# Low-rank projections on unnormalised x, a narrow rotary key, merged query rotary parts and a router on VectorE, in a two-layer diffusion step

## What is computed

```
h = rmsnorm(x) * (1 + scale) + shift           # scale, shift from the conditioning
z = h @ w_in  ->  qd, kd, vd (512 each), cq (256), ckv (128), kr (32)
q_mla = rmsnorm(cq) @ w_uq                      # 4 heads x (64 plain + 32 rotary)
ckv   = rmsnorm(ckv); kr = rotary(kr)           # kr is one key part, shared by 4 heads
diff  = softmax(q1 k1) - lam * softmax(q2 k2), times v      # 4 heads
mla   = softmax(qn (ckv w_uk) + qr kr) (ckv w_uv)           # 4 heads
x = x + gate * ([diff, mla] @ w_o)
h = rmsnorm(x) * (1 + scale) + shift
x = x + gate * ffn(h)       # layer 0: SwiGLU 2816 wide; layer 1: best 2 of 8 experts
```

## Time and profile before

| | |
|---|---|
| median of 3 runs | 2214.25 us (2213.64 to 2216.69) |
| profiled execution | 2219.65 us, span 2218.0 us |
| busy in the span | TensorE 95%, its weight loads 83%, VectorE 61%, ScalarE 52%, GpSimd 6% |
| mean granted TensorE clock | 0.987 |
| layer 0 begins, layer 1 begins, router, experts, end | 0, 901, 1291, 1333, 2158 us |

### The profile page before, as it was taken

One profiled execution on the slowest core, in us unless ns is written; L12 is line 12 of the kernel. 1 busy time (PEld: TensorE's weight loads), 2 busy tenths in 40 slices (PEclk: granted clock), 3 DMA queues, 4 the chain that ended last, 5 costly groups with the idle time before them and its releaser, 6 DMA issues. The chain is left out here.

```text
span 2218.0 us, 32258 instructions
## 1 busy us (share of the span) xinstructions
PE 2115.1 (95%) x12409; PEld 1836.0 (83%) x12409; DVE 1353.8 (61%) x1447; ACT 1143.0 (52%) x1419; POOL 127.0 (6%) x147
## 2 busy tenths in 40 slices
PE   5999899999999999899999988999999999999996
PEld 2998567999999999798856877888888888888885
DVE  4427443644423443543843367989998998998884
ACT  3316453322212222422844336787777887877763
POOL 0130100000000000022010030000000000000001
PEclk8999999999999999999999989999999999999998
DMA  8320045256432212312015219999999999999964
GB/s 286 100 83 6 1 152 188 81 164 206 138 91 77 77 55 71 113 58 64 6 39 190 96 68 393 386 387 387 387 387 386 386 387 387 386 387 386 386 247 143
DMA packets 281711, 455.41 MB, mean 205 GB/s; under 512 B 12368, under 2 KB 160720, under 8 KB 281616
## 3 DMA queue, kind: packets, MB, share of 16 engines
q1 hardware_dynamic: 267040, 419.74, 53.8%
q0 software_dynamic: 7920, 28.84, 3.3%
q10 hardware_dynamic: 6656, 5.47, 0.8%
HBM read 426.07 MB, written 27.95 MB: 205 GB/s over the span
## 5 line engine op out<-in xcount | busy, mean ns | idle before, releaser
L1655 DVE TENSOR_TENSOR w_lo<-mraw,w_hi 128x1792 fp32r<-128x1792 f32 (+2 forms) x306 | 642.7, 2111 | 92.6 <-ACT w_hi L1095 91.3
L1095 ACT ACTIVATE w_hi<-mraw 128x1792 fp32r<-128x1792 f32 (+2 forms) x306 | 541.8, 1775 | 189.6 <-PE ps L2272 156.6
L2270 PE MATMUL ps<-w_hi,xs_lo 128*128 128x448 f32 (+1 forms) x816 | 311.2, 381 | 7.3 <-DVE w_lo L1655 6.6
L2272 PE MATMUL ps<-w_hi,xs_hi 128*128 128x448 f32 (+1 forms) x816 | 305.9, 375 | 0.0
L2271 PE MATMUL ps<-w_lo,xs_hi 128*128 128x448 f32 (+1 forms) x816 | 305.6, 375 | 0.0
L1203 DVE TENSOR_TENSOR sub_lo<-zone,sub_hi 128x1024 fp32r<-128x1024 f32 (+2 forms) x114 | 132.0, 1159 | 268.7 <-ACT sub_hi L802 268.6
L802 ACT ACTIVATE sub_hi<-zone 128x1024 fp32r<-128x1024 f32 (+2 forms) x114 | 111.2, 978 | 145.5 <-PE ps L1898 98.8
L2270 PEld LDWEIGHTS ps<-w_hi,xs_lo 128*128 128x128 f32 x816 | 153.7, 188 | 34.0 <-DVE w_lo L1655 14.9
L2272 PEld LDWEIGHTS ps<-w_hi,xs_hi 128*128 128x128 f32 x816 | 153.6, 188 | 19.7
L2271 PEld LDWEIGHTS ps<-w_lo,xs_hi 128*128 128x128 f32 x816 | 153.8, 189 | 18.4
L1375 DVE TENSOR_REDUCE stat<-ps 128x2 f32<-128x1536 f32 (+3 forms) x80 | 92.4, 1157 | 114.1 <-PE ps L1982 97.5
(11 more groups left out here) (291 smaller groups left out, 3566.4 us busy)
## 6 DMA issues: line engine op xcount, KB each, us to landing
mraw<-in_moe_w_down SPq DMA_DIRECT2D x68, 1024.0 KB, 13.6
mraw<-in_moe_w_gate SPq DMA_DIRECT2D x68, 896.0 KB, 13.1
mraw<-in_moe_w_up SPq DMA_DIRECT2D x68, 896.0 KB, 13.3
zone<-in_w_ada SPq DMA_DIRECT2D x48, 1024.0 KB, 5.9
mraw<-in_moe_w_gate SPq DMA_DIRECT2D x34, 1024.0 KB, 14.4
mraw<-in_moe_w_up SPq DMA_DIRECT2D x34, 1024.0 KB, 14.3
mraw<-in_moe_w_down SPq DMA_DIRECT2D x34, 768.0 KB, 13.4
zone<-in_w_in SPq DMA_DIRECT2D x14, 1024.0 KB, 5.4
```

Source lines behind the costliest of these rows:

```text
L1095: nc.scalar.activation(w_hi[:, n % SPLITS, a], mraw[:, n % MRING, a], ACT.Copy).then_inc(w_hi_ready, 1)
L1655: nc.vector.tensor_tensor(w_lo[:, n % SPLITS, a], mraw[:, n % MRING, a], w_hi[:, n % SPLITS, a].bitcast(f32), ALU.subtract).then_inc(w_spl ...
L2270: nc.tensor.matmul(out, a_lo, b_hi, start=start, stop=False)
L2272: return nc.tensor.matmul(out, a_hi, b_hi, start=False, stop=stop)
```

## The change

It does five things.

1. In layer 1 the three low-rank labels take gain times x, which ScalarE and VectorE write chunk by chunk behind the down projections; `make_gain(1, 0)` moves ahead of these. The token sums stand between chunks 4 and 5 of the first label. VectorE multiplies by the token factor as it reads PSUM (`low_rank_scaled`), ScalarE adds the shift (`low_rank_shifted`). `keep_busy` goes. The norm and its split parts are still made, for the labels that follow, and `("rope", 1, 0)` takes them chunk by chunk. In layer 1 the loads of small weights and caches go from ScalarE's queue to GpSimd's.
2. The rotary key is no padded label any more: `key_part` does 32-wide float32 matmuls in four column groups, `key_sums` adds the groups and rotates, VectorE finishes (`key_rope`).
3. The query weights are reordered so that the plain parts of two heads share one label of 128 (`uq`), and the rotary parts of all four heads another (`("rope", l, 8)`, finished by `query_rope`). The `uk` labels cover two heads each. GpSimd copies the key part to the four heads.
4. In the router the five masks become one operation, the shift additions go from GpSimd to VectorE, between its other steps.
5. The router's softmax goes behind the experts.

The diff, cut to its core:

```diff
+            m(("rope", l, r), "raw_ready", 9 * l + r + 1)
+            if r == 0:
+                m(("kr", l), "kr_copied", l + 1)
+            if r == 1:
+                m(("kr_sum", l), "kr_summed", l + 1)
...
-        for h in range(4):
-            x(("rot", l, 9 + h), "rot_used", 13 * l + 10 + h)
-        for r in range(9, 13):
-            m(("rope", l, r), "raw_ready", 13 * l + r + 1)
-        for h in range(4):
-            m(("uk", l, h), "km_ready", 4 * l + h + 1)
+        x(("rot", l, 8), "rot_used", 9 * l + 9)
+        m(("rope", l, 8), "raw_ready", 9 * l + 9)
+        for g in range(2):
+            m(("uq", l, g), "uq_out", 2 * l + g + 1)
+        for g in range(2):
+            m(("uk", l, g), "km_ready", 4 * l + 2 * g + 2)
...
+        def small_weights_in(eng, l):
+            eng.dma_start(wkr, w_in[l, :, :, 1920:1952]).then_inc(layer_w_in[l], 16)
+            eng.dma_start(wuq, d["w_uq"][l].rearrange("(k p) n -> p k n", p=P)).then_inc(layer_w_in[l], 16)
+            eng.dma_start(wuk, d["w_uk"][l]).then_inc(layer_w_in[l], 16)
+            eng.dma_start(wuv, d["w_uv"][l]).then_inc(layer_w_in[l], 16)
+        def caches_in(eng, l):
+            eng.dma_start(ckv_t[:, 0:PAST], d["cache_ckv"][l]).then_inc(cache_c_in[l], 16)
+            eng.dma_start(kr_t[NOPE:MQK, 0:PAST], d["cache_kr"][l]).then_inc(cache_c_in[l], 16)
+            eng.dma_start(k_t[:, :, 0:PAST], d["cache_k"][l]).then_inc(cache_k_in[l], 16)
+            eng.dma_start(v_n[:, 0:2, :], d["cache_v"][l]).then_inc(cache_v_in[l], 16)
         block = ctx.enter_context(nc.Block())
...
             for l in range(DEPTH):
-                for r in range(13):
+                if l:
+                    pool.wait_ge(late_turned, TURNS_BEFORE[l])
+                    pool.wait_ge(main_done, MAIN[("lora", l, 0)] + 1)
+                    small_weights_in(pool, l)
+                    pool.wait_ge(main_done, MAIN[("lora", l, 2)] + 1)
+                    caches_in(pool, l)
+                for r in range(8):
                     rope_item(l, r)
+                pool.wait_ge(kr_done, l + 1)
+                pool.wait_ge(cache_c_in[l], 16 * N_CACHE_C)
+                pool.wait_ge(kv_out, 16 * 4 * (l + 1))
+                pool.wait_ge(scores_done, (2 * l + 1) * ITEMS)
+                for h in range(HEADS):
+                    nc.gpsimd.tensor_copy(k_t[NOPE:MQK, h, :], kr_t[NOPE:MQK, :]).then_inc(kr_spread, 1)
...
-                pool.wait_ge(shift_row_ready, 2)
-                pool.wait_ge(htok_scaled, t + 1)
-                nc.gpsimd.tensor_tensor(htok[:, t, :], htok[:, t, :], shift_row[t // (TT - 1)], ALU.add).then_inc(htok_ready, 1)
...
+                    sub_hi_part(q + 3)
                 else:
...
                     root(4 * l + 1)
                     act.wait_ge(zero_rows, 16 * 2 * XTILES)
-                    modulate(1, 1, 0)
...
+                    modulate(1, 1, 0, ks=range(3))
+                    sub_hi_part(q + 3)
+                    modulate(1, 1, 0, ks=range(3, KC))
+                    sub_hi_part(q + 4)
+                def low_rank_shifted(g):
+                    act.wait_ge(lora_scaled, g + 1)
+                    for c, (a, b) in enumerate(((0, N_LAT), (N_LAT, T))):
+                        ins = nc.scalar.activation(lora_raw[:, g, a:b], lora_raw[:, g, a:b], ACT.Identity,
+                                                   bias=shift_part[:, g // 2, g % 2, c:c + 1])
+                    ins.then_inc(lora_ready, 1)
...
-                    raw_item(l, r)
+                act.wait_ge(scores_done, (2 * l + 1) * ITEMS)
+                for g in range(2):
+                    act.wait_ge(main_done, MAIN[("uq", l, g)] + 1)
+                    for c in range(2):
+                        ins = nc.scalar.activation(q_t[0:NOPE, 2 * g + c, :], main_pair(("uq", l, g))[NOPE * c:NOPE * c + NOPE, :],
+                                                   ACT.Copy, scale=-M_SCALE)
+                    ins.then_inc(uq_out, 1)
...
+                                if d_ == 0:
+                                    act.wait_ge(gain_ready, 4)
+                                for c, (a, b) in enumerate(((0, N_LAT), (N_LAT, T))):
+                                    ins = nc.scalar.activation(f_hi[:, d_, a:b], x_t[:, d_, a:b], ACT.Copy, scale=gain[:, 1, 0, d_, c:c + 1])
+                                ins.then_inc(h_hi_ready, 1)
...

...
+                kr_ps = main_pair(("kr_sum", l))[rows]
+                nc.vector.tensor_copy(kr_t[rows, PAST + N_LAT:NKEY], kr_ps[:, N_LAT:T])
+                nc.vector.tensor_tensor(kr_t[rows, PAST:PAST + N_LAT], kr_ps[:, 0:N_LAT], cos_m[rows, :], ALU.mult).then_inc(kr_summed, 1)
+                dve.wait_ge(aux_done, AUX[("kr_rot", l)] + 1)
+                nc.vector.tensor_tensor(kr_raw[rows, 0:N_LAT], AUXP[rows, 0:N_LAT], sin_m[rows, :], ALU.mult).then_inc(kr_rotated, 1)
+                dve.wait_ge(kr_rotated, l + 1)
+                dve.wait_ge(kr_summed, l + 1)
+                nc.vector.tensor_tensor(kr_t[rows, PAST:PAST + N_LAT], kr_t[rows, PAST:PAST + N_LAT], kr_raw[rows, 0:N_LAT],
+                                        ALU.add).then_inc(kr_done, 1)
...
+            def query_rope(l):
+                n = 9 * l + 8
+                dve.wait_ge(raw_ready, n + 1)
+                dve.wait_ge(rope_done, n)
+                link(nc.vector.tensor_tensor(rtmp[:, (n + 1) % 2, :], raw[:, n % 2, 0:N_LAT], cos_m[:], ALU.mult))
+                rot(l, 8)
+                dve.wait_ge(rot_used, n + 1)
+                dve.wait_ge(scores_done, (2 * l + 1) * ITEMS)
+                for h in range(HEADS):
+                    rows = slice(ROPE * h, ROPE * h + ROPE)
+                    ins = nc.vector.tensor_tensor(q_t[NOPE:MQK, h, 0:N_LAT], rtmp[rows, 0, :], rtmp[rows, 1, :], ALU.add)
+                ins.then_inc(rope_done, 1)
 
...
+                def low_rank_scaled(g):
+                    m = MAIN[("lora", 1, g)]
+                    dve.wait_ge(main_done, m + 1)
+                    nc.vector.tensor_tensor(halves(lora_raw[:, g, :]), main_halves(("lora", 1, g)), halves(rb[:]), ALU.mult)
+                    o = 1024 * (m % 3) + 512 + TH
+                    nc.vector.tensor_copy(shift_part[:, g // 2, g % 2, :], ps[:, o:o + 2]).then_inc(lora_scaled, 1)
+                def beside_norm(k):
+                    if k == 2:
+                        low_rank_scaled(0)
+                    if k == 5:
+                        sub_rest(q + 3)
+                    if k == 7:
+                        low_rank_scaled(1)
                 if l:
                     sub_rest(q + 2)
-                    norm(2 * l, l, 4 * l + 1, ("norm", l, "mix"), 16 * l)
-                sub_rest(q + 3)
-                sub_rest(q + 4)
...
-                    if h == 0:
-                        dve.wait_ge(rope_done, 13 * l + 9)
-                        dve.wait_ge(cache_c_in, 16 * N_CACHE_C * (l + 1))
-                    nc.vector.tensor_copy(k_t[NOPE:MQK, h, :], kr_t[NOPE:MQK, :]).then_inc(kr_spread, 1)
...
+                        if half:
+                            dve.wait_ge(mod_late, TURNS_BEFORE[1])
+                            make_gain(1, 0)
+                            nc.vector.drain().then_inc(gain_ready, 1)
                         for d_ in range(KC):
                             for _ in range(2):
                                 q += 1
@@ -1560,9 +1633,13 @@
                             residual(l, ("down", half, d_), d_, 40)
                             if half and d_:
                                 add_square(1, "mix", d_ - 1)
+                                scaled_rest(d_ - 1, 1, 0)
+                            if half and d_ == 1:
+                                dve.wait_ge(shift_hi, 2)
+                                nc.vector.tensor_tensor(f_lo[:, :, T:TX], mod[:, 1, 0:8, :], f_hi[:, :, T:TX].bitcast(f32),
+                                                        ALU.subtract).then_inc(shift_split, 1)
                     add_square(1, "mix", KC - 1)
-                    dve.wait_ge(mod_late, TURNS_BEFORE[1])
-                    make_gain(1, 0)
+                    scaled_rest(KC - 1, 1, 0)
 
...
+            def add_shift(t):
+                dve.wait_ge(htok_scaled, t + 1)
+                dve.wait_ge(shift_row_ready, 2)
+                nc.vector.tensor_tensor(htok[:, t, :], htok[:, t, :], shift_rows[t], ALU.add).then_inc(htok_ready, 1)
...
+            link(nc.vector.tensor_tensor(flat(cmp_b[:]), flat(cmp_b[:]), small[:, 0:64].unsqueeze(1).to_broadcast([P, TT, NE * NE]), ALU.mult))
             link(nc.vector.tensor_tensor(flat(cmp_a[:]), flat(cmp_a[:]), flat(cmp_b[:]), ALU.add))
             link(nc.vector.reduce_sum(rt[:, 1], cmp_a[:], AXX))
...
-                project_group([("lora", l, g) for g in range(3)], (h_split, 16 * l),
-                              beside=lambda k: None if l else last_sums(k))
-                project(("rope", l, 0))
+                if l == 0:
```

(37 more changed lines are left out.)

301 lines of the change are left out of this document (143 added, 158 removed).

## The result

| | before | after |
|---|---|---|
| median of 4 timed runs | 2214.59 us (2213.64 to 2216.69) | 2196.89 us (2195.30 to 2200.97) |
| ratio, 95% interval | | 0.9921 (0.9906 to 0.9935) |
| profiled execution | 2219.65 us, span 2218.0 | 2197.08 us, span 2195.5 |

The kernel became faster by 17.7 us, less than half of the 37.8 forecast, and outside the range of 2168 to 2190. The question is where the other 20 us went.

The account below looks back on a forecast made before the run. The prediction took TensorE, busy 95% of the span, as the bound, with its gaps before the expert stage to be shortened. Its terms, -18.4 + 0.4 - 1.6 - 8.8 - 9.4 = -37.8 us, took 2214.25 to 2176.5, range 2168 to 2190.

Parts of the forecast that it names:

- Step 2: Rotary key, both layers: narrow matmuls replace a projection and a rotation; -1.6 us in layer 0, +0.4 in layer 1.
- Its last sentence: Signs of being wrong: narrow cross-partition operations costing several times more, late GpSimd loads, or TensorE's clock lowered at new places.
- Step 3: Passage from differential to latent attention, both layers: -5.9 us each, 1.5 given back to GpSimd's copies; -4.4 a layer, -8.8.
- Step 1: Join of the two layers: low-rank projections start without waiting for the norm, -18.4 us; `rope 0` then waits 1.5 us.
- Step 4: Router: one mask operation and additions on VectorE start the DMA stream earlier; -9.4 us, between -5 and -11.
- rival B: Router's gain doesn't reach the experts: held scatters or the sixth piece leave stream gaps, 2 us of 9.4 left; 2184, 10%.
- Step 5: End: router softmax behind the last expert, about 5 us, covered by TensorE's wait for gathered rows; costs nothing.
- The base: Profiled execution of before, 2219.65 us, was 5.4 above the timed median, 2214.25; the forecast difference was applied to the median.
- A: Passage gives about -1 us a layer instead of -4.4, from GpSimd holding VectorE or dearer narrow additions; 2183, 15%.
- E: The join keeps its gap because first chunks or their shift columns come late: -19 us, 2195; 5%.
- F: Slower: the key part waits for four small loads on GpSimd's queue; at 65 us to landing, 2218; 3%.

Follow-up runs that it names:

- v1: Changed kernel with the second value-weight split on ScalarE ahead of its copy of the last rotary item, both layers: 2186.08 us, ratio to before 0.9870.
- v4: Changed kernel with the router's arithmetic put back (five masks, shift additions on GpSimd, softmax before the experts): 2207.01 us, ratio 0.9959.
- v5: v1 with TensorE's sums of the ckv squares ahead of the narrow key matmuls, both layers: 2186.09 us.
- v11: v1 with VectorE's reciprocal in the second layer's first norm done three times, 8.3 us more: 2198.90 us, ratio 0.9913.
- v7: v1 with GpSimd's four copies of the rotated key held until VectorE has combined the last differential attention item: 2183.91 us, ratio 0.9852.
- v6: v1 with VectorE's four key copies ahead of the four narrow query additions in both passages: 2181.28 us, ratio 0.9842.
- v8: v1 with throw-away matmuls, three and one, in the two stalls of each passage: 2183.47 us, ratio 0.9853.
- v9: Changed kernel with the edits of v1, v5, v6 and v7 together: 2173.26 us, ratio 0.9803.
- v10: v9 without the new order of the sums of the ckv squares: 2173.95 us, ratio 0.9821.

## Why the prediction was wrong

**Step 2, the rotary key, is the step that failed, by a term that the sum puts at nothing.** It says "-1.6 in layer 0, +0.4 in layer 1" and counts only what the removed label does itself: a projection, a rotation, the matmuls in their place. It does not ask what the missing label does to the order in which ScalarE splits weights. The second piece of the value weights came to stand behind the copy of the last rotary item, and that copy waits for GpSimd, VectorE and TensorE in turn. The value stretches, for which the sum has no term, grew by 5.8 and 6.8 us, 12.6 together; v1, which puts this split ahead of the copy again, gave 10.8 us back. The removed projection itself was not what covered the chain: it ended at 78, some 67 us ahead of layer 0's value matmuls, and the last copy comes as late against them in both kernels. The prediction's rule to name the cover of each edit that costs nothing was applied to what was added, and not to the order of what stayed. Its last sentence named the right danger, a clock lowered at new places, but put neither place nor price to it.

The key part itself was sized well for its matmuls (4.8 us measured with its drain, 4.5 forecast). But in layer 0 step 2 cost time where it should have given 1.6 us. The forecast missed two waits, 1.45 us for a bank and 1.02 for a variance, made by the key matmuls that hold up the sums. Behind the first four projections, whose number and size the change leaves alone, the way to the first value matmul took 68.7 us, before 67.2 and 67.0: 1.5 us more. The table's 0.8 us less comes from these four projections: 34.2 and 34.1 us in the two profiles of before, where the clock is lowered from 38.6, and 31.8 after, where it is not. Three profiles of changed kernels with the clock lowered there, v4, v5 and v11, have 33.5, 34.5 and 33.4.

**Step 3, the passage.** Forecast -5.9 a layer with 1.5 given back in attention. The 1.5 was near (0.8 and 1.0; 1.3 in v1) and was GpSimd's copies holding VectorE, as v7 shows. The Trainium skill, "SBUF — State Buffer", section "SBUF: two separate sides", says that the pair of ports shared by VectorE and GpSimd is an exclusive lock for a whole instruction, also against a VectorE operation with two SBUF inputs; the trace agrees, with 0.70 and 0.97 us in place of 0.22 and 0.35. The passages gave 4.1 and, by the mean of two profiles of before, 2.5. In layer 1, 23.8 us less the clock's share is 19.8, against 19.3 forecast. That share is 1.4 us on the first two projections, which start 2.13 and 1.42 us apart where 1.08 is usual, and 5.49 - 2.84 = 2.65 on the last value matmuls. So the count of instructions held, and the missing term is the clock. v6 and v8 show that the short stalls bring the later part of it; the earlier part starts ahead of the passage.

**Step 1, the join, was right.** Forecast -18.4 + 0.4 = -18.0, measured -18.5 (743.5 to 725.0). By the forecast the last low part comes at 931.5 and `rope 0` waits 1.5 us; in v1 it waits 0.69. v11 confirms that this is the edge of the cover.

**Step 4, the router, was right, and a little small.** Forecast -9.4, between -5 and -11. The stretch gained 12.2, of which the router is 10.9 (v4). The ten scatters took 14.6 us in all, 3.3 more than before, where the forecast allowed 5; that did not reach the experts, so rival B falls.

**Step 5, the end, was right:** the softmax is covered (v4).

**The base.** I applied the difference to the median of the timed runs. The stretches add up to -0.8 + 12.6 + 1.8 - 6.6 - 18.5 - 12.2 = -23.7 us without start and end, and the medians differ by 17.7. Both profiles of before took longer than the median of the runs beside them, by 5.1 and 5.4 us; the one of after took 0.2 us more than its own. So about 6 us of what the profiles show as gain is not there between the timed runs. Of these, 2.3 are the clock in the first four projections. What else varies I can name (start 3.2, end 3.0, passage of layer 1 2.2), but not why it fell that way in the profiles: 3.7 us stay open.

The 20.1 us that the forecast missed are then: value stretches 12.6, passages with attention 4.0 (-4.8 instead of -8.8), rotary key in layer 0 3.1, less 0.5 for the join and 2.8 for the router's stretch, and these 3.7.

Of the rivals, A (the passage gives little) happened in part, in layer 1. E's 2195 us lies near the measured time by luck: the gap that it keeps is gone. F did not happen: the small loads were issued from 908.3 to 911.3 and nothing waited for them. The rival that was missing is "a removed label changes the order of what stays, and a split comes too late", and it was the largest.

## What to carry to other kernels

When an item leaves a sequence that several engines share, write down for each of them how many items ahead it prepares, before and after, and follow the last items up to where their results are needed. A queue that runs in order can hold a split that is needed soon behind a copy that waits for a third engine, as ScalarE's did here; one place in the order was worth 10.8 us. And where TensorE's work is broken by short waits, give each a price of its own in the forecast for the clock behind it: here waits of 1 to 4 us cost between half as much and as much again.

## What I had not expected of the hardware

- A wait of 3.84 us was followed by 3.4 us of lowered clock in one layer and 6.8 in the other, with the same instructions; by the growth of the stretches over the wait that cost 1.9 and 3.0 us.
- In the passage a stall costs more than its length. Taking 2.3 us of stall away gave 4.1 and 4.8 us, and filling the stalls with useless matmuls gave 1.7 and 2.5.
- The clock was fully up in one passage of v9 and of v10 and not in the other, in alternate layers. In v8, v9 and v10 it was lowered again at the end of the latent attention that follows, between 340 and 355 us, where v1's was not. Whether and where it falls thus also hangs on something that these edits do not set.
- GpSimd's copies of 32 x 896 took 0.90 us each, under half of the 2.0 that the forecast took as their upper bound. The other way round, in v1 an addition on GpSimd took 2.13 us beside the value split that now runs at that time on VectorE, and 1.27 without it.
